# Weight strips handed over in halves between ScalarE, GpSimd and TensorE, in a two-block sequence model on one core

## What is computed

```
first_block:   u = rms_norm(h);  proj = u @ w_in
               y_hy = hyena(short_conv(proj...))      y_ml = bidirectional mLSTM(q, k, v, gates)
               h += concat(y_hy, y_ml) @ w_out
               h += cross_attention(rms_norm(h), rms_norm(mem))
               h += square(relu(rms_norm(h) @ ff_w1)) @ ff_w2
second_block:  h = rmsnorm(x);  b_a, c_a, x_a, x_b, g_b, gate_a, gate_b = split(h @ w_in)
               y_a = b_a * causal_conv(c_a * x_a)
               y_b = rg_lru(causal_conv(x_b)) * gelu(g_b)
               x += (sigmoid(gate_a + ..) * (y_a @ w_out_a) + sigmoid(gate_b + ..) * (y_b @ w_out_b)) @ w_o
               x += (silu(h @ w_ffn_gate) * (h @ w_ffn_up)) @ w_ffn_down
```

## Time and profile before

| | before |
|---|---|
| median of 3 runs | 1902.72 us (1899.79 to 1903.24) |
| profiled execution | 1900.95 us, span 1898.9 us |
| TensorE busy | 1763.8 us, 93% |
| GpSimd busy | 751.6 us, 40%, in 312 instructions |
| ScalarE busy | 633.9 us, 33% |
| VectorE busy | 971.0 us, 51% |
| granted TensorE clock, mean | 0.966 |

### The profile page before, as it was taken

One profiled execution on the slowest core, in us unless ns is written; L12 is line 12 of the kernel. 1 busy time (PEld: TensorE's weight loads), 2 busy tenths in 40 slices (PEclk: granted clock), 3 DMA queues, 4 the chain that ended last, 5 costly groups with the idle time before them and its releaser, 6 DMA issues.

```text
span 1898.9 us, 21690 instructions
## 1 busy us (share of the span) xinstructions
PE 1763.8 (93%) x7718; PEld 1424.0 (75%) x7718; DVE 971.0 (51%) x1285; ACT 633.9 (33%) x789; POOL 751.6 (40%) x312
## 2 busy tenths in 40 slices
PE   6899998885799898999999999999999999999996
PEld 4677875663678686888888877777888888888885
DVE  5752387888862447242334676767323343133136
ACT  3322342232242341122114456566333343222222
POOL 3342441113334143444444345455444444444442
PEclk9899998987899998999999999999999999999998
DMA  4232221111222022222222323232222222222222
GB/s 160 89 111 78 89 86 37 34 45 45 89 89 89 23 92 75 100 90 98 99 97 91 103 97 111 99 100 99 90 99 99 96 93 99 97 91 100 100 91 97
DMA packets 47695, 169.28 MB, mean 89 GB/s; under 512 B 5205, under 2 KB 5205, under 8 KB 47321
## 3 DMA queue, kind: packets, MB, share of 16 engines
q1 hardware_dynamic: 44640, 160.45, 24.6%
q10 hardware_dynamic: 3000, 8.09, 1.2%
HBM read 166.43 MB, written 2.10 MB: 89 GB/s over the span
## 4 chain that ended last, share of the span: by engine, by line
PE 29%; issue 29%; POOL 14%; DVE 1%; POOLq 0%; ACT 0%; DVEq 0%
POOL m_w_lo L439 14%; PE ps L471 10%; PE ps L473 10%; PE ps L472 10%; DVE m_h L1948 0%; DVE m_s L1209 0%; POOLq L447 0%; POOLq L445 0%; POOL m_QL L459 0%; DVE m_qs L1581 0%; PE ps L499 0%; DVE m_qs L1583 0%; DVE m_ftmp L1573 0%; DVE m_ftmp L1571 0%; DVE m_s L1923 0%
## 5 line engine op out<-in xcount | busy, mean ns | idle before, releaser
L439 POOL TENSOR_TENSOR m_w_lo<-m_raw,m_w_hi 128x1024 fp32r<-128x1024 f32 x302 | 737.2, 2444 | 1073.0 <-ACT m_w_hi L881 1072.8
L881 ACT ACTIVATE m_w_hi<-m_raw 128x1024 fp32r<-128x1024 f32 x302 | 318.1, 1056 | 652.6 <-DMA m_raw<-in_strips 648.9
L471 PE MATMUL ps<-m_XH,m_w_hi 128*128 128x512 f32 x1160 | 470.7, 406 | 10.6 <-POOL m_w_lo L439 8.8
L472 PE MATMUL ps<-m_XL,m_w_hi 128*128 128x512 f32 x1160 | 455.6, 393 | 0.0
L473 PE MATMUL ps<-m_XH,m_w_lo 128*128 128x512 f32 x1160 | 455.4, 393 | 0.0
L471 PEld LDWEIGHTS ps<-m_XH,m_w_hi 128*128 128x128 f32 x1160 | 220.4, 190 | 75.9 <-POOL m_w_lo L439 17.5
L472 PEld LDWEIGHTS ps<-m_XL,m_w_hi 128*128 128x128 f32 x1160 | 220.6, 190 | 46.6 <-issue 2.4
L473 PEld LDWEIGHTS ps<-m_XH,m_w_lo 128*128 128x128 f32 x1160 | 220.1, 190 | 47.2
L471 PE MATMUL ps<-m_FH,m_w_hi 128*128 128x512 f32 x432 | 169.1, 391 | 2.9 <-DVE m_FL L1202 2.8
L472 PE MATMUL ps<-m_FL,m_w_hi 128*128 128x512 f32 x432 | 168.7, 390 | 0.0
L473 PE MATMUL ps<-m_FH,m_w_lo 128*128 128x512 f32 x432 | 168.6, 390 | 0.0
(11 more groups left out here) (310 smaller groups left out, 2260.1 us busy)
## 6 DMA issues: line engine op xcount, KB each, us to landing
m_raw<-in_strips SPq DMA_DIRECT2D x302, 512.0 KB, 3.2
m_x_in<-in_x ACTq DMA_DIRECT2D x8, 256.0 KB, 4.3
m_x_res<-in_x ACTq DMA_DIRECT2D x1, 2048.0 KB, 8.0
out<-m_h SPq DMA_DIRECT2D x8, 256.0 KB, 2.1
m_memf<-in_mem ACTq DMA_DIRECT2D x1, 1024.0 KB, 10.2
m_decay<-in_decay ACTq DMA_DIRECT2D x1, 1024.0 KB, 14.9
m_w<-in_w ACTq DMA_DIRECT2D x1, 512.0 KB, 13.3
m_skip<-in_skip ACTq DMA_DIRECT2D x1, 512.0 KB, 3.7
```

The costliest lines, as they stand in the source:

```text
L439: nc.gpsimd.tensor_tensor(w_lo[:, c], raw[:, c], f(w_hi[:, c]), ALU.subtract).then_inc(lo_ready, 1)
L471: pe.matmul(dst, w_hi[:, c], xh, start=first, stop=False)
L472: pe.matmul(dst, w_hi[:, c], xl, start=False, stop=False)
L881: act.activation(w_hi[:, c], raw[:, c], ACT.Copy).then_inc(hi_ready, 1)
```

## The change

ScalarE makes the high part in two ACTIVATEs of 128 x 512, each counted in `hi_ready`; GpSimd makes the low part in two subtractions of 128 x 512, each with its own wait for `hi_ready` and its own count in `lo_ready`; `strip` waits for the first half before contraction tile 0 and for the second before tile 4. All other waits for `lo_ready` ask for both halves (the count doubled). Loads, slots and the order of all other work stay.

```diff
@@ gpsimd
-            def low(slot):
-                c = slice(slot * STRIP, (slot + 1) * STRIP)
-                nc.gpsimd.tensor_tensor(w_lo[:, c], raw[:, c], f(w_hi[:, c]), ALU.subtract).then_inc(lo_ready, 1)
+            def low(slot, before):
+                for part in range(2):
+                    pool.wait_ge(hi_ready, before + (part + 1))
+                    c = slice(slot * STRIP + part * (STRIP // 2), slot * STRIP + (part + 1) * (STRIP // 2))
+                    nc.gpsimd.tensor_tensor(w_lo[:, c], raw[:, c], f(w_hi[:, c]), ALU.subtract).then_inc(lo_ready, 1)
...
-                            pool.wait_ge(hi_ready, i * RING + (first + u + 1))
-                            low((first + u) % RING)
+                            low((first + u) % RING, i * (2 * RING) + 2 * (first + u))
@@ tensor, strip
-                pe.wait_ge(lo_ready, n + 1)
+                pe.wait_ge(lo_ready, n * 2 + 1)
...
                 for k in range(kt):
+                    if k == KT // 2:
+                        pe.wait_ge(lo_ready, n * 2 + 2)
@@ tensor, six other places
-                    pe.wait_ge(lo_ready, n + 1)
+                    pe.wait_ge(lo_ready, (n + 1) * 2)
@@ scalar, high
-                c = slice(slot * STRIP, (slot + 1) * STRIP)
-                act.activation(w_hi[:, c], raw[:, c], ACT.Copy).then_inc(hi_ready, 1)
+                for part in range(2):
+                    c = slice(slot * STRIP + part * (STRIP // 2), slot * STRIP + (part + 1) * (STRIP // 2))
+                    act.activation(w_hi[:, c], raw[:, c], ACT.Copy).then_inc(hi_ready, 1)
```

More of the change, by code:

```diff
@@ L446, in lows @@
                         for u in range(RING):
-                            pool.wait_ge(hi_ready, i * RING + (first + u + 1))
-                            low((first + u) % RING)
+                            low((first + u) % RING, i * (2 * RING) + 2 * (first + u))
                 for n in range(end - rest, end):
-                    pool.wait_ge(hi_ready, n + 1)
-                    low(n % RING)
+                    low(n % RING, 2 * n)
             lows(0, S_HY + N_HY)
@@ L722, in _ @@
             for u in range(4):
-                pe.wait_ge(lo_ready, S_WOUT + u + 1)
+                pe.wait_ge(lo_ready, (S_WOUT + u + 1) * 2)
                 for k in range(4, KT):
@@ L832, in in_turn @@
                     n = v * 6 + 5
-                    pe.wait_ge(lo_ready, i * 12 + (S_IN + n + 1))
+                    pe.wait_ge(lo_ready, (i * 12 + (S_IN + n + 1)) * 2)
                     pe.wait_ge(u_pair, mt + 1)
```

## The result

The changed kernel takes **1876.61 us** (median of 4 runs, 1872.49 to 1877.85) against 1902.49 of the kernel before on the same chip: ratio 0.9863, 95% interval 0.9844 to 0.9881. The profiled span is 1876.0 us.

A forecast was written before the change was run, and what follows sets the result against it. The prediction took the ScalarE-VectorE loop to set the LRU turn. Gains of 8.8 (LRU), 1.1 (behind it), 0.6 (K and V) and 1.2 (mLSTM) made 11.7 us, from 1902.7 to 1891.0 us; range 1884 to 1904.

The forecast's parts named there:

- The bound and the loop: LRU stage: ScalarE and VectorE, waiting for each other, set the 31.08 us turn; TensorE's waits for lows are an echo.
- forecast turn: LRU stage: a turn was to take 30.0 us, not 31.08 and not 28.5.
- stage gain: LRU stage: eight taps stretches and seven passes from gelu to the next turn, 8.8 us gained together.
- the walk: LRU loop followed op by op with halves of 1.25 us: gains of 0.19 at BL, 0.28 behind xtap, 0.86 behind uH.
- The price of a half: GpSimd's 128x512 low, called H: 1.25 us taken, with 1.20 as lower bound and 1.45 as upper end.
- The 1.35: Rival: a GpSimd half has 0.3 us fixed, so H = 1.35; gain 4.5 us, 1898.2 us; chance 0.14.
- mLSTM: mLSTM stage: L1444 is free after the first half, 0.8 us less, four times; 1.2 us counted.
- K and V: Two waits in K and V that ask for both halves of two strips: 0.3 us each, 0.6 together.
- Behind the LRU stage: TensorE's 0.97 us wait for a low at 1320.71 goes, 1.1 us gained.
- The gain is mostly the 0.42 us of the earlier start and a single op that slips between halves: LRU loop: GpSimd starts 0.42 us earlier after the first high half; this and one op slipping between halves gives most gain.
- TensorE's second wait: 257 strips get one more wait in their middle; it should cost nothing, being met with a margin of 0.9 us.
- The rival with TensorE at its own pace: Rival: TensorE's waits vanish and it sets the pace; turn 28.5 us, gain 14 to 16 us, 1887; chance 0.05.

The follow-up runs named there:

- e1: The changed kernel, but TensorE waits for both low halves before a strip's first tile: 1875.08 us, ratio 0.9869.
- e2: The changed kernel, but ScalarE makes the high in one piece, with the low still in halves: 1867.66 us, ratio 0.9828.
- e7: The changed kernel, but GpSimd's first low half waits for both halves of the high: 1869.55 us, ratio 0.9830.
- e12: The changed kernel with halves only for strips in front of the first feed-forward stage, whole from there on: 1890.65 us, ratio 0.9946.
- e8: The kernel before, plus ten matmuls with unread results in front of the first feed-forward down part: 1901.99 us in one run.
- e11: A bound against the kernel before: GpSimd makes one contraction tile's low per strip, TensorE uses it for all eight, high whole: 1816.30 us, ratio 0.9554.

## Why the prediction was wrong, step by step

**The bound and the loop: right.** The LRU turn is set by ScalarE and VectorE, not by TensorE's waits. Shown by e1: TensorE gets its weights later, and the turn stays at 30.0. The forecast turn (30.0) and stage gain (8.8 us) came out at 30.02 and 8.6. From xtap's start to the second tap's end it is now 5.07 us where it was 5.25, from uH's end to yA's 7.15 where it was 8.09: gains of 0.18 and 0.94, where the walk had 0.28 and 0.86.

**The price of a half: nearly right.** 1.25 taken from the memset row, 1.29 measured at the median, 1.26 at the least. By the prediction's own slope (0.8 us a turn for 0.1 us of H) a half of 1.29 would have left 6.2 of the 8.8 us in the LRU stage; 8.6 came, so that the stage's number fits so well is partly luck. The 1.35 was an estimate of the prediction, from the 4497 ns for 2048 elements in the Trainium skill's "GPSIMD Engine Reference", section 3.1, and this trace's 2398 ns for 1024. The halves, quarters and eighths here (1294, 741, 463 ns) lie on a line of 2.16 ns an element with 0.19 us fixed, and the trace does not agree with the estimate's 0.30 fixed.

**The step that failed: the terms outside the LRU stage were put at almost nothing.** The prediction said that where VectorE's ops come thick each half blocks one of them. It costed the mLSTM stage at 1.2 us, K and V at 0.6, and the hyena and feed-forward stages not at all. For the hyena stage no reason was given; the feed-forward stage was taken as free of idle time from a window that starts at 757.00, behind TensorE's 2.81 us wait for FL. In the profiled execution:
- mLSTM: 1.2 forecast, 5.8 measured (4.8 to 9.2 in e1, e2, e7 and e12, which have halves there too). TensorE's waits for `m_s` fell by 3.6 us alone, and its busy time from 103.6 to 101.0 with the clock up from 0.90 to 0.92.
- Hyena: 0 forecast, 2.6 (2.2 to 5.1 in those runs).
- First feed-forward (from 698.80, the start of its first up part): 0 forecast, 3.3; I had said nothing of the 2.81 us wait for FL, half of whose gain is clock (e8).
- K, V and the projections: 0.6 forecast, 1.8.
- Behind the LRU stage: 1.1 forecast, 1.0.

Together these are 2.9 forecast and 14.5 measured. The median's 26 us are some 3 more than the traces' 23; which stage they belong to stays open.

**The reading of the gain was wrong too: "The gain is mostly the 0.42 us of the earlier start and a single op that slips between halves".** The first part has the wrong sign. The earlier start costs 7 us by the medians (e7) and 10 of the LRU stage in the traces, since it lets the low catch `BH` and the first tap as well. The walk had both ops behind a half, correctly, and so the LRU sum came out; but it was never walked with halves and the later start. What carries the gain is the size of the piece that VectorE waits for: halves 26 us (34 with the later start of e2), quarters 48, eighths 59, of the 85 of e11.

**TensorE's second wait costs nothing: right**; e1, without it, is no faster, and the feed-forward stage with it takes the same 267.9 us. But the earlier hand-over brings nothing either, beyond 1.0 us at one place.

**The range.** Its lower end was H = 1.20, as if the price of a half were the one thing open. The rival with TensorE at its own pace (1887) came true in e2 and not in the change. No rival said that VectorE's waits outside the LRU stage mattered, though the page had VectorE at 971 us for work that takes 784 (e11).

## What to carry to other kernels

Where one engine's instructions wait for another engine's running one, as VectorE's here for GpSimd's, look first at the waiting engine's durations against its shortest for the same form. What is above is waiting: it is booked as busy time, and no view of waits shows it. It is worth something only in stages where the bounding engine waits for that engine. Then cut the other engine's instruction to the smallest piece whose fixed part still leaves it time (here 128x128, 0.46 us; with pieces half as large a strip took 5.2 of the 5.44 us that TensorE gives it). And walk the start of such an instruction in both directions before splitting what feeds it: earlier can be worse.

## What the runs showed of the hardware

- GpSimd's two-input subtraction of fp32 with 128 partitions took 2.40 us for 1024 elements, 1.29 for 512, 0.74 for 256, 0.46 for 128 and 0.32 for 64 (medians). All five lie within 0.01 us of 0.19 us and 2.16 ns an element.
- A single-source VectorE op from SBUF (`BH`, TENSOR_SCALAR, 0.43 us) waits for a running low like one with two sources (1.40 us in the change), while ops with a PSUM source don't: in the kernel before, 157 TENSOR_TENSOR of 128x512 with one of two sources in PSUM lay wholly beside running lows and took 0.68 to 0.69 us, where the 92 with no low beside them took 0.67 to 0.69. I had the first in my walk, but not that delaying a low by 0.4 us avoids it.
- After a wait of 2.81 us TensorE went on at the lower clock for 3.5 us; after 3.33 us (e12) at the lower clock for 5.7 us; after 1.04 and 1.29 us it kept the upper one.
